# Output projections and second FFN products with tokens on partitions, and norms from per-token sums of squares

## The reference

```python
for layer in range(2):
    mod = silu(c) @ ada_w[layer] + ada_b[layer]
    sh_m, sc_m, g_m, sh_f, sc_f, g_f = split(mod, 6)
    h = rms_norm(x, norm_w[layer, 0]) * (1 + sc_m) + sh_m
    y = even_mixer(h, ...) if layer == 0 else odd_mixer(h, ...)   # each ends in y @ w_out
    x = x + g_m * rms_norm(y, norm_w[layer, 1])
    h = rms_norm(x, norm_w[layer, 2]) * (1 + sc_f) + sh_f
    y = conv_ffn(h, ...)      # h @ w_in, 3-tap conv, a * gelu(g), @ w_out
    x = x + g_f * rms_norm(y, norm_w[layer, 3])
```

## Time and profile before

| | us |
|---|---|
| median of 3 runs | 2669.17 (2665.86 to 2672.18) |
| the profiled execution, its own time | 2670.19 |
| its span, first to last instruction | 2668.3 |
| PE busy | 2466.6 (92% of the span) |
| DVE busy | 2020.0 (76%) |
| ACT busy | 1078.5 (40%) |
| POOL busy | 462.8 (17%) |

### The profile page before, as it was taken

The page is one execution under the profiler, slowest core; times in us unless marked ns, Lnnn a source line. Parts: engine busy times, 40 slices in busy tenths (PEclk is TensorE's granted clock), DMA queues, the critical chain, the costliest instruction groups (busy, mean ns, idle before and its releaser), DMA issues.

```text
span 2668.3 us, 47925 instructions
## 1 busy us (share of the span) xinstructions
PE 2466.6 (92%) x18998; PEld 2389.3 (90%) x18998; DVE 2020.0 (76%) x2394; ACT 1078.5 (40%) x1111; POOL 462.8 (17%) x230
## 2 busy tenths in 40 slices
PE   1399998979999999999979999988999999999997
PEld 1398877969999999999979989987999999999997
DVE  7877887779987999789777766677998456645655
ACT  1334334454333333333464544544434333433344
POOL 0100000013430344024210000000444024401420
PEclk7699998989999999999989999989999999999998
DMA  9887774857778777887757644366577455555453
GB/s 397 327 318 288 280 248 148 278 180 262 270 280 317 288 268 278 309 297 270 251 190 263 227 154 147 142 233 237 209 274 260 174 188 175 187 175 186 178 182 132
DMA packets 114781, 631.37 MB, mean 237 GB/s; under 512 B 12752, under 2 KB 12880, under 8 KB 62944
## 3 DMA queue, kind: packets, MB, share of 16 engines
q1 hardware_dynamic: 114656, 629.61, 64.8%
HBM read 627.46 MB, written 2.10 MB: 236 GB/s over the span
## 4 chain that ended last, share of the span: by engine, by line
PE 81%; DVE 9%; DMA 5%; ACT 2%; issue 2%; POOL 1%; DVEq 0%; SPq 0%; ACTq 0%; POOLq 0%
PE bank L1422 24%; PE bank L1423 23%; PE bank L1424 23%; DMA piece<-ada_pieces 3%; PE bank L1441 2%; PE bank L1443 2%; PE bank L1442 2%; DVE lo L805 1%; DVE region L816 1%; DMA region<-ada_pieces 1%; PE bank L1329 1%; DVE piece L816 1%; ACT hi L439 1%; DVE act L866 1%; DVE region L836 1%
## 5 line engine op out<-in xcount | busy, mean ns | idle before, releaser
L1422 PE MATMUL bank<-act,hi 128*128 128x256 f32 x4384 | 1261.3, 288 | 112.3 <-DVE act L866 96.8
L439 ACT ACTIVATE hi<-raw 128x2048 fp32r<-128x2048 f32 x402 | 769.6, 1915 | 1301.9 <-PE bank L1424 1174.6
L1423 PE MATMUL bank<-act,hi 128*128 128x256 f32 x4384 | 1247.9, 285 | 0.0
L1424 PE MATMUL bank<-act,lo 128*128 128x256 f32 x4384 | 1247.6, 285 | 0.0
L805 DVE TENSOR_TENSOR lo<-raw,hi 128x2048 fp32r<-128x2048 f32 x402 | 920.8, 2290 | 193.6 <-ACT hi L439 192.7
L1422 PEld LDWEIGHTS bank<-act,hi 128*128 128x128 f32 x4384 | 849.1, 194 | 122.3 <-issue 108.0
L1423 PEld LDWEIGHTS bank<-act,hi 128*128 128x128 f32 x4384 | 849.7, 194 | 1.0
L1424 PEld LDWEIGHTS bank<-act,lo 128*128 128x128 f32 x4384 | 849.0, 194 | 0.0
L816 DVE SCALAR_TENSOR_TENSOR piece<-piece,cond 128x1024 f32<-128x1024 f32 x320 | 451.4, 1411 | 78.2 <-DMA piece<-ada_pieces 77.9
L1422 PE MATMUL bank<-mid,hi 128*128 128x256 f32 x1408 | 406.6, 289 | 13.3 <-POOL mid L789 13.3
L1423 PE MATMUL bank<-mid,hi 128*128 128x256 f32 x1408 | 400.5, 284 | 0.0
(11 more groups left out here) (150 smaller groups left out, 1516.6 us busy)
## 6 DMA issues: line engine op xcount, KB each, us to landing
raw<-w_units SPq DMA_DIRECT2D x402, 1024.0 KB, 4.8
piece<-ada_pieces SPq DMA_DIRECT2D x320, 512.0 KB, 4.8
region<-ada_pieces SPq DMA_DIRECT2D x64, 512.0 KB, 8.7
x<-x_in SPq DMA_DIRECT2D x1, 2048.0 KB, 16.3
x_out<-x SPq DMA_DIRECT2D x4, 512.0 KB, 2.6
cond<-c_row SPq DMA_DIRECT2D x1, 1024.0 KB, 4.9
vec<-vectors SPq DMA_DIRECT2D x1, 534.5 KB, 11.8
extra<-blocks_in SPq DMA_DIRECT2D x1, 512.0 KB, 18.4
```

The source lines that it names most:

```text
L439: sc.activation(hi[:, slot, :], raw[:, raw_slot, :], ACT.Copy).then_inc(s_hi, 1)
L1422: pe.matmul(dst, w_hi, src[:, kt, 0:T], start=at == 0, stop=False)
L1423: pe.matmul(dst, w_hi, src[:, kt, T:2 * T], start=False, stop=False)
L1424: i_ = pe.matmul(dst, w_lo, src[:, kt, 0:T], start=False, stop=at == len(order) - 1)
```

## The change

`mixed` and `ff_down` use `tokens`. In `mixed` a body of 8 units makes two output tiles of 512 channels in turn, so that units 0 and 1 need only the first four of 16 activation tiles, units 2 and 3 the next four, and so on; the gating work of `gate_tail` is spread over these units (`gate_work`). The third `ff_down` has 12 units and not 16 (394 in all). `x` and `y` are held with tokens on partitions, so a token's squares are summed by ACT's accumulator (Square with `accum_out`), and no product with ones is left in these norms. Before the next product PE transposes `x` by a product with a diagonal matrix that holds the reciprocal root of each token; ACT and DVE then apply alpha and shift in one step, alternately, in pairs of tiles; POOL has no part. Gamma is now needed along the free axis: ACT writes it to DRAM as a row of 2048 single values and reads it back broadcast (1 MB), four times in all. The residual is one instruction per part instead of two, in five parts. The pieces are dealt out anew: 32 (24 before) in the first columns phase, 16 (24) in each `mixed`, 16 (8) in the third `ff_down` of layer 0. In the last body of the mLSTM the norm of its result moves into the output projection.

```diff
+    def token_unit(self, j):
+        if self.kind == "mixed":
+            return j % 2, tail(self)[0][j // 2], j < 2, j >= 6
+        tile, g = divmod(j, self.k_units)
+        return tile, g, g == 0, g == self.k_units - 1
...
-              Phase("columns", 0, 4, 4, (2, 1, 2, 1), dest=FQ),
+              Phase("columns", 0, 4, 4, (2,) * 4, dest=FQ),
...
-              Phase("mixed", 0, 4, 4, (2, 1, 2, 1)),
+              Phase("mixed", 0, 2, 8, (0, 1, 0, 0, 1, 2, 2, 2)),
...
+              Phase("ff_up", 0, 6, 4, (1,) * 4, 2), Phase("ff_down", 0, 1, 12, (1, 2, 1) * 4, 2),
...
+              Phase("mixed", 1, 2, 8, (0, 0, 0, 0, 1, 2, 2, 3)),
...
+X_PIECES = ((0, 0, 1024), (0, 1024, 1024), (1, 0, 1024), (1, 1024, 512), (1, 1536, 512))
...
+            def square_x(q):
+                for k, (tb, at, size) in enumerate(X_PIECES):
...
+                    sc.activation(yt[:, tb, at:at + size], x[:, tb, at:at + size], ACT.Square,
+                                  accum_out=stat[:, col:col + 1]).then_inc(s_xsq, 1)
...
+            def gamma_row_dmas(ph, j):
+                m = 2 * ph.layer + int(ph.kind == "ff_down")
+                if j == 5:
+                    sc.wait_ge(s_gamma, m + 1)
+                    with nc.allow_non_contiguous_dma("2048 values, once for each norm"):
+                        sc.dma_start(row_dram.rearrange("a (k p) -> p (a k)", p=P), gamma[:, :]).then_inc(s_row_out, 16)
+                if j == 6:
+                    sc.wait_ge(s_row_out, 16 * (m + 1))
+                    sc.dma_start(gamma_row, row_dram.broadcast_to([P, D])).then_inc(s_row, 16)
...
+            def x_root(q):
+                rho = stat[:, S_RHO:S_RHO + TB]
+                ve.wait_ge(s_xsq, len(X_PIECES) * (q + 1))
+                ve.tensor_reduce(rho, split2(stat[:, S_X:S_X + 3 * TB]), AX_X, ALU.add).then_inc(s_mean, 1)
+                rooted(rho)
...
+                for tb in range(TB):
+                    i_ = ve.tensor_scalar(diag[:, tb, :], ident[:, :], rho[:, tb:tb + 1], None, ALU.mult)
...
+                def scaled(p):
+                    ve.wait_ge(s_tp, 8 * q + p + 1)
+                    for kt in (2 * p, 2 * p + 1):
+                        i_ = ve.tensor_scalar(y[:, kt, :], bank[4 + p % 4][:, (kt % 2) * T:(kt % 2 + 1) * T],
+                                              alpha[:, kt:kt + 1], mod[:, sh, kt:kt + 1], ALU.mult, ALU.add)
...
+            def by_gamma(ph, chunk, first=0, last=TB):
...
+                ve.tensor_tensor(yt[:, first:last, at], yt[:, first:last, at],
+                                 gamma_row[:, at].unsqueeze(1).broadcast_to([P, last - first, 512]),
+                                 ALU.mult).then_inc(s_yg, 1)
...
+            def post_norm(ph, between):
...
+                by_gamma(ph, CHUNKS - 1, 0, 1)
+                ve.wait_ge(s_ysq, TB * CHUNKS * (m + 1))
+                ve.tensor_reduce(r, split2(stat[:, S_Y:S_Y + TB * CHUNKS]), AX_X, ALU.add).then_inc(s_mean, 1)
+                by_gamma(ph, CHUNKS - 1, 1, 2)
+                between()
+                rooted(r)
...
+                for tb, at, size in X_PIECES:
+                    x_at = x[:, tb, at:at + size]
+                    ve.scalar_tensor_tensor(out=x_at, in0=yt[:, tb, at:at + size], scalar=r[:, tb:tb + 1], in1=x_at,
+                                            op0=ALU.mult, op1=ALU.add).then_inc(s_x, 1)
...
+            def x_transposes(q, p):
...
+                for kt in (2 * p, 2 * p + 1):
+                    for tb in range(TB):
+                        at = (kt % 2) * T + tb * P
+                        i_ = pe.matmul(bank[4 + p % 4][:, at:at + P], x[:, tb, kt * P:(kt + 1) * P], diag[:, tb, :],
+                                       start=True, stop=True)
+                i_.then_inc(s_tp, 1)
...
+                    if ph.kind == "mixed" and first_body(i) and tile == 0:
+                        pe.wait_ge(s["gated_lo_ready"], 4 * ph.layer + j // 2 + 1)
                     for q in range(4):
-                        kt = 4 * (j % 4) + q
+                        kt = 4 * group + q
+                        if ph.kind == "ff_down" and first_body(i) and tile == 0:
+                            pe.wait_ge(s_mid, ph.pairs - FF_GROUPS[ph.group] + kt + 1)
...
-                        if ph.sums and not (first_body(i) and j == 0):
-                            sum_y_square(ph.units * i + j - 1, (j + 1) % 2)
+                        if ph.kind == "mixed" and ph.layer == 1 and first_body(i) and j == 1:
+                            gla_sums(G_HEADS)
```

More of the change, by code:

```diff
@@ L64, in __init__ @@
         self.per_body = sum(ada)
-        self.tiles = units // 4 if kind == "values" else units
+        self.k_units = len(range(0, FF_GROUPS[group], 4)) if kind == "ff_down" else 4
+        self.tokens = kind in ("values", "mixed", "ff_down")
+        self.tiles = units // self.k_units if self.tokens else units
         self.sums = kind == "mixed" or (kind == "ff_down" and group == len(FF_GROUPS) - 1)
@@ L497, in pre_norm @@
[L497 to L506 removed]
+                        sc.wait_ge(s_x, len(X_PIECES) * (q - 1) + k + 1)
@@ L1144, in _ @@
                     gate_tail(ph)
-                if ph.sums:
-                    gate_weight(ph.layer, int(ph.kind == "ff_down"))
+                if ph.kind == "ff_down" and ph.sums:
+                    gate_weight(ph.layer, 1)
                 def body(i, ph=ph):
@@ L1166, in body @@
                         after_split(ph, i, j)
+                        if ph.kind == "mixed" and first_body(i):
+                            gate_work(ph, j)
+                            if j == 4:
+                                gate_weight(ph.layer, 0)
+                        if ph.kind == "columns" and ph.side == "gla" and i == ph.bodies - 1 and j == ph.units - 1:
+                            mixer = PHASES[PHASES.index(ph) + 1]
+                            gate(mixer, 0)
+                            gate(mixer, 1)
                         if ph.ada[j] > 0:
@@ L1515 @@
         w = (even_out_w, odd_out_w)[layer][0]
-        for m in range(DK):
-            units[n] = columns_unit(w, slice(m * P, (m + 1) * P))
-            n += 1
+        rows = row_units(w)
+        mixer = next(ph for ph in PHASES if ph.kind == "mixed" and ph.layer == layer)
+        for i in range(mixer.bodies):
+            for j in range(mixer.units):
+                chunk, group = mixer.token_unit(j)[0:2]
+                units[n] = rows[mixer.tiles * i + chunk, group]
+                n += 1
         first = 0
@@ L1525 @@
                     n += 1
-            rows = ffn_out_w[layer][first * P:(first + tiles) * P]
-            for m in range(DK):
-                units[n][:, 0:tiles * P] = columns_unit(rows, slice(m * P, (m + 1) * P))
-                n += 1
+            got = row_units(ffn_out_w[layer][first * P:(first + tiles) * P]).reshape(-1, P, UNIT)
+            units[n:n + len(got)] = got
+            n += len(got)
             first += tiles
```

584 lines of the change are left out of this document (307 added, 277 removed).

## The result

The changed kernel takes 2651.47 us (median of 7 executions, 2643.85 to 2658.95), the kernel before, on the same chip, 2667.44 (7 executions, 2659.65 to 2672.18): ratio 0.9938, 95% interval 0.9918 to 0.9958. It is faster by 16 us, 0.6%: clear of noise, but a sixth of the 97 that were forecast, and outside the range 2550 to 2600. The profiled execution after took 2654.36 with a span of 2652.6, 15.7 less than the span before.

A forecast was written before the change was run, and what follows sets the result against it. PE's pace inside the phases plus the chains at their edges bound the kernel. Terms of -53, -29.6, -14.3, -5.2, -2, +6 and +1 sum to -97, from 2668.3 to 2571 us; range 2550 to 2600, about 8 in 10.

The forecast's parts named there:

- The pace: Second FFN products and output projections: a token unit takes 5.44 us, not 5.76, 38 us of the 97.
- the rival by which the form is worth nothing: Token units elsewhere take the 5.76 us of a columns unit, so all 38 us are lost, 2609; 4%.
- Head: Start of the run: only the chain from alpha to the first unit shortens, -2 us.
- end: After the last product: updates and last store take 12.6 us for 17.8, -5.2.
- Gamma's row: Write of 2048 single values, four times: up to 9 us costs nothing, 31 costs 22; taken as +1 us.
- The rival with this mechanism: Gamma's row takes near 31 us a time, giving 2659, within 0.5% of the old time; 2%.
- the start and 9 of stalls: Output projections: about 2.8 us before unit 0 and 9 of stalls a phase, for 99 and 99.5 us.
- The pieces: First columns phase: two pieces a unit through two slots cost +6 us, bounds 0 to 31.
- The rival of this name, slower than before: A piece's round through two slots decides; gain gone at landing of 6.8 us, 2710 at 7.5; 3%.
- the term of `ff_down`: Second FFN products: 478.7 us for 533.6, plus 2 where DVE's work falls together, -53.
- The edges: Three edges to a norm of `x`: 30.5, 28.5 and 31 us for 36.7, 34.1 and 33.5, -14.3.
- The rival with 17%: Gating and transposes eat the edges: projections stall 20, not 9, edges stay 33 to 34; 2588 to 2604; 17%.

The follow-up runs named there:

- e2: Changed kernel with gamma's row written one phase earlier and read back from unit 2 of the phase that uses it; 2600.9 us, ratio 0.9735.
- e7: Changed kernel with gamma's row written as 128 runs of 64 bytes, not 2048 single values, nothing moved; 2627.64 us, ratio 0.9842.
- e3: Changed kernel with SP's wait for the last GLA head moved behind the fourth unit load of layer 1's output projection; 2634.61 us, ratio 0.9866.
- e5: Changed kernel with the edits of e2, e3 and e4 together; 2585.73 us, ratio 0.9684.
- e4: Changed kernel with eight pieces dealt from the first columns phase to the mLSTM phase; 2632.55 us, ratio 0.9853.
- e6: Kernel before with only the new deal of pieces in the first columns phase and layer 0's output projection; 2687.04 us, ratio 1.0071.
- e10: e8 with layer 1's projection pieces dealt (0,0,0,1,2,2,2,1), not (0,0,0,0,1,2,2,3); 2582.55 us, ratio 0.9690.
- e8: Changed kernel with the edits of e5 and e7 together; 2586.91 us, ratio 0.9691.

## Why the prediction was wrong

**Right.** The pace: token units take 5.44 us, and the rival by which the form is worth nothing falls. The waits for `mid` went: a token `ff_down` has its first unit after 5.36 us, where it was 6.9 to 9.3. The first product of `mixed` came as early as worked out. Head -2.4 (forecast -2), end -5.3 (-5.2).

**Gamma's row, the step that failed most.** The term was +1, resting on "the next split it could delay is due some 9 us after the issue, so a write of up to 9 us costs nothing". Two things were wrong. The deadline was read off ACT alone; DVE's product with gamma stands right behind the first tile's evacuation, 6.6 us after the issue (2592.2 against 2585.6), and it needs the write and the read, one after the other: 13.9 + 7.7 = 21.6 us. And the size, 14 us, was in the stated bounds of nothing to 31 but was taken at "nearer the low end". e2 puts the price at 52 us of span, the slow clock behind the stalls in it, of which the prediction had no term. The rival with this mechanism had 2% and was priced at ACT's wait only; its 2659 came near the measured time by chance, as it took other causes besides this one to get there. The Trainium skill (DMA: Bandwidth & Descriptors, section Rules for kernel authors) advises to rearrange so that the last dimension is contiguous; e7 agrees, 4.5 us for 14.2, medians of four.

**SP's list, a step that was missing.** The prediction counted ACT's and DVE's lists in the projections and left SP's out, although it says itself that queues are strict lists. The last head's norm moved behind the mixer, so what SP waits for is there only 29 us into the projection (1754.8 against 1725.96), and unit loads stand behind it. e3 prices it at 11.8 us in that projection. The forecast stood 12.0 and 12.5 us above 16 pure units (the start and 9 of stalls); the change stands 19.7 (106.7 less 87.0) and 35.7 above them. With both causes gone it is 11.0 and 14.5 in e5: the term's size was near for what it counted, and two causes were left out.

**The pieces, a term whose size was off.** +6, measured +12.0 in the first columns phase and +4.1 in the next (2 to 7 in the five traces of this deal). The formula, sum 1.25, landing, 0.2, was taken with L = 4.8; with the 5.3 that the loads took there it gives 6.75 a unit, and 6.5 was measured. A longer L belongs to a denser queue, and the prediction only put that in its upper bound. DVE has 5.3 us of its own work in such a unit (2.29, two pieces of 1.30, 0.42), which leaves no slack to recover in. e4 and e6 show the cost from both sides; that the round and not the DMA engines' capacity sets it is argued by this formula only. The rival of this name, slower than before, needed L of 6.8 and did not come: the three `ff_down` of layer 0 take 3 to 6 us each more than those of layer 1 in e5, where the row is early. That is 13.3 us together, where the term of `ff_down` had put 2.

**The edges.** -14.3 forecast, -9.2 measured, most of the gap in the last one: 34.1 for 31. DVE's timeline shows where. The last product is at 1848.67. The split of a unit and a piece stand ahead of the last evacuation, which starts at 1851.28 and not at once, two more pieces stand behind it, and the last of them is 1.70 us late; the first update begins at 1859.66, 11.0 after the product, where 5.3 + 2.5 was worked out.

```profile
1851.28 1.28 DVE L1306 COPY y<-bank 128x512 f32<-128x512 f32 x2
...
1853.61 1.22 DVE L862 SCALAR_TENSOR_TENSOR piece<-piece,cond 128x1024 f32<-128x1024 f32 x1
...
1856.54 1.23 DVE L862 SCALAR_TENSOR_TENSOR piece<-piece,cond 128x1024 f32<-128x1024 f32 x1 [1.70 <-DMA piece<-ada_pieces]
...
1859.66 5.00 DVE L965 SCALAR_TENSOR_TENSOR x<-y,stat,x 128x1024 f32<-128x1024 f32 x5
```

**The rival with 17%,** stalls of 20 in each projection and edges of 33, 2588 to 2604, described the projections best, but its cause was another: not too much work in DVE's list, but DMAs that landed late or went out late.

Where the 81 us between forecast and span went, by the runs: in single edits from the change's span of 2652.6, gamma's row 51.7, SP's order 14.6, the deal 14.4. The three together give 62.5, 18 less than their sum. Stage by stage, 10 are the mLSTM phase, which got the write and the eight pieces at once (79.3, where the single edits would add up to 69.7), 8 the two projections, and 6 the values phase beside attention, which differs by 3 us between executions as said; the other stages give 6 back. The profiled executions of e3 and e4 are the slowest of their four; by the ratios the single gains are 54, 19 and 23 us and the three together 68, so the overlap is 28. Between e5 and the forecast 19 us are left: 7 in `ff_up` (nearly all the write's), 6 in `ff_down` and 5 in the edges, the rest in ones and twos. The forecast's mixer phases hold 6 us for a deal that e5 no longer has, so against the kernel before they are 7 too long.

## What to carry to other kernels

A small DMA is priced from both ends: how long from issue to landing, with every transfer chained behind it, and which engine's list needs it first, not only the list that issued it. When a producer is moved later, look through every queue, the one that only issues loads included, for waits on it that stand ahead of loads which don't need it. A slot that fits its round exactly has no slack: cost it with the landing time of the denser queue that the change makes.

## What the runs showed of the hardware

An 8 KB write of 2048 single values took 11.0 to 13.9 us with only unit loads beside it, and 10.8 to 22.0 with pieces too (the 22.0 in e4, in the last `ff_down` of layer 0); as 128 runs of 64 bytes it took 1.4 to 5.5 (e7 to e10). It slows its neighbours: in the mLSTM phase of e5 it took 13.7 us, the four loads issued from 0.5 us before it to 11 us after took 9.8 to 14.6, and that phase went back from 79.3 to 72.4 with the short form, where such loads took 4.8 to 5.0 (e8).

DVE reads float32 values 64 bytes apart more slowly than neighbours: 1.93 us for 1.22 on 1024 values, 1.02 for 0.68 on 512 (e7). The Trainium skill (SBUF — State Buffer, section Door 1: The DMA port swizzle) says that SBUF has lines of 16 bytes, so that float32 can be stepped over by four values at most for free. By that rule, the trace agrees: a step of 16 costs 58%. No run has a step between 1 and 16, and the product's pattern has one dimension more in e7, so the step alone isn't isolated.
